# The last attention stage in pairs of heads, on halves of the TensorE array

## The chip, the cores and the metric

The kernel runs on one core of one Trainium2 chip. The metric is the device time of one launch in microseconds; a lower time is better. Everything is held in float32, and weights go to the array as a rounded part and a remainder (fp32r).

## The reference, cut to what matters

Two transformer layers follow one another on 512 tokens of width 1024. The first has a sparse and a windowed attention, the second a latent and a stick-breaking attention, and the third stage of attention, the one that is changed, is a causal softmax attention with forget gates: 16 heads of 64, for which

```python
q, k, v, gate logits = split(x @ w_in)          # 3 x 1024 + 16 columns
q, k   = rms_norm per head, times a gain of 64
decay  = cumsum(log_sigmoid(logits + f_bias))   # per head, over the tokens
s      = q @ k.T / 8 + decay[query] - decay[key]
p      = softmax(where(key <= query, s, -1e30))
out    = (p @ v) @ w_o
```

A feed-forward part closes each layer. The decay of the query is the same for all keys of a row, so a softmax does not see it.

## The kernel before, in words

The kernel is one program per engine, written in the order in which each engine runs it, with semaphores between them. TensorE (PE) does the products and transposes, ScalarE (ACT) copies and exponentials, VectorE (DVE) reductions and copies, GpSimd (POOL) splits each weight slab into high and low part (`split_slab`, two operations of 128x1024), SyncE issues the weight loads. Each phase (`in1`, `cmp`, ..., `in3`, `out3`, `up3`, `down3`) walks over slabs of weights; four slots hold split slabs.

`in3` projects to the queries, gate logits, keys and values of the last attention. Each chunk of 512 columns lands in `tok3` by tokens, is normed per head on DVE (`head_norms`), gets two more columns for the decays (`decays_beside`, so a head has 66), and is turned head by head by `pe_turn` (L603) into `qf` and `kf`, 66 rows by 512 tokens; ACT (L1189) and DVE (L1618) empty the banks in turn, with the gain.

The attention itself (`pe_attend`, `act_attend`, `dve_attend` with `att["fox"]`) goes over 16 heads, and in each over four blocks of 128 queries, the longest first: 512, 384, 256 and 128 keys. For each step PE forms the scores (L875; a float32 product is two loads of weights and two passes), adds the causal mask with a bf16 product (L880), three steps later turns the probabilities in blocks of 128x128 (L887), and then multiplies them with the values (L896, 64 columns out). DVE takes the negated row maximum (L1709), ACT the exponential with its sum (L1285) and the copy of the turned probabilities (L1298), DVE the inverse of the sum and the scaled result (L1730, L1923). POOL copies the queries of the next head into `q_st` (L456).

The result stands in `v3` by tokens. `pe_out` then turns it (L721, 32 transposes, name `x3`), ACT and DVE make the high and low part in `xt_hi` and `xt_lo` (L1122, L1550), and `out3` multiplies with the weights (L588 to L590).

At the very start `small_loads` has ACT issue 18 small loads; DVE waits for all of them (L1776), forms the rotation angles, ACT takes their sines, and only then ACT copies the first projected tiles (L1374).

Of the kernel before, what the change touches and what calls it, by code (L numbers as in the profile page):

```python
# [14 lines left out]
P = 128  # L15
SEQ = 512
D = 1024
NT = SEQ // P
# [8 lines left out]
TOKW = 528  # L27
# [3 lines left out]
SMALLS = 18  # L31
# [49 lines left out]
def build(nc, A, out):  # L81
# [17 lines left out]
    NORMS = ["n0", "n1", "n3", "n5", "x2", "n6", "n7", "x3", "n8"]  # L99
# [46 lines left out]
    band = sb("band", [P, P], BF16)  # L146
    one = sb("one", [P, 1])
# [13 lines left out]
    m_cos = sb("m_cos", [P, NT, ROPE])  # L161
    m_sin = sb("m_sin", [P, NT, ROPE])
# [68 lines left out]
    qf = sb("qf", [HD + 2, 16, SEQ], F32, u)  # L231
    kf = sb("kf", [HD + 2, 16, SEQ], F32, u)
# [5 lines left out]
    decay = sb("decay", [P, NT, 16], F32, u)  # L238
    u.close()
# [9 lines left out]
    red = sb("red", [P, NT, ROPE // 2], F32, u)  # L249
    u.close()  # L250
# [196 lines left out]

    def stage_queries(e, ph, q_src, rows, iters, ready, before=None):
# [25 lines left out]
    def _(e):  # L474
# [47 lines left out]
        e.wait_ge(consts, 19)  # L522
# [27 lines left out]
    def mla_heads(dst, h0, which):  # L550
# [14 lines left out]
    T_IN3 = [alternate([(66 * i, 66, (qf, kf)[c // 2][:, 8 * (c % 2) + i, :]) for i in range(8)],  # L565
                       g_col[0:66, 2 + c // 2:3 + c // 2]) for c in range(4)] + [[], []]
# [146 lines left out]
    def pe_to_xt(e, name, src, ready, t):  # L713

        e.wait_ge(*ready(t))
        for q in range(2):
            i = 2 * t + q
            if i >= 4 and name in ("n1", "x2", "x3"):
                e.wait_ge(*at(f"{name}_lo", i - 3))
# [49 lines left out]
    def pe_pairs(e, name, c, s0, kts, x_of, last, turn, when):  # L769
# [4 lines left out]
        for pair in ((0, 1), (2, 3)):  # L774
            for s, kt in enumerate(kts, s0):
# [4 lines left out]
                if pair[0] == 2:  # L780
                    m.then_inc(slab_used, 1)
                    for t in when.get(s - s0, ()) if turn else ():
                        turn(t)

# [78 lines left out]

    def pe_attend(e, cfg):
# [57 lines left out]
        with e.Fori(0, iters - 1) as j:  # L922
# [16 lines left out]
        "fox": dict(name="fox", iters=8, look=3, dh=HD + 2, band=False, mask=causal,  # L939
                    k=lambda hd: heads(kf, hd), v=lambda hd: columns(v3, hd),  # L940
                    start=[at("in3_tpa", 16), at("in3_tpd", 16), at("in3_copy", 23)], banks=[at("in3_copy", 24)]),
# [3 lines left out]
    def _(e):  # L945
# [108 lines left out]
        def decays():  # L1054

            e.wait_ge(*at("consts", 20))
# [6 lines left out]

        def turn_first():
            e.wait_ge(*at("fox_dec_out", 1))
# [5 lines left out]
                   "n7", turn("n7"), {(2, 0): turn_logits, (2, 1): decays, (2, 3): turn_first})  # L1071
        pe_attend(e, att["fox"])
# [967 lines left out]
```

## Time and profile before

| what | value |
|---|---|
| median of 3 runs | 2260.43 us (2259.78 to 2261.72) |
| span of the profiled execution | 2259.5 us |
| that execution's own time | within the runs' 2259.78 to 2261.72 us; the page gives its span alone |
| PE busy | 2103.5 us, 93% of the span |
| POOL, DVE, ACT busy | 1071.8, 894.1, 582.4 us |
| chain that ended last | PE 87%, DVE 7%, ACT 2% |
| last attention stage | 1745.5 to 1840.1 us |

A time is read from the start of the span. The length of an instruction includes its way through the engine; what one costs in a row of its kind is the distance from start to start. PE is the matmul itself, PEld the load of its weights, which can lie beside the matmul before.

### The profile page before, as it was taken

How to read it: one execution, taken by the hardware profiler on the slowest of the kernel's cores; microseconds unless marked ns; L12 is line 12 of the kernel's file. 1: busy time of each engine (PE TensorE's matmuls, PEld its weight loads, DVE VectorE, ACT ScalarE, POOL GpSimd, SP SyncE). 2: the span in 40 equal slices, each digit the busy share in tenths (PEclk: the TensorE clock that was granted, in tenths of full speed). 3: DMA queues.
4: the chain of work that ended last, by engine and by line, in shares of the span. 5: the costliest groups of instructions: out<-in, count | busy, mean ns of one | idle time of the engine just before them, and what ended most of it. 6: DMA issues, size and time to landing. Idle time of an engine off the chain costs nothing.

```text
span 2259.5 us, 30914 instructions
## 1 busy us (share of the span) xinstructions
PE 2103.5 (93%) x10410; PEld 1715.7 (76%) x10420; DVE 894.1 (40%) x1703; ACT 582.4 (26%) x1432; POOL 1071.8 (47%) x688
## 2 busy tenths in 40 slices
PE   5776999789999989879999999999999999999999
PEld 4665676678888878766678888887787888888887
DVE  4663567264434015546654221201362644221200
ACT  2111556232222003336532011100132642011100
POOL 4443003257666655400135666665553036666664
PEclk9887998889999999988579999999999999999999
DMA  4222001113333322110012333332221013333322
GB/s 132 66 61 66 0 0 38 47 57 111 93 95 119 93 77 82 54 38 1 0 47 84 103 98 97 93 94 84 79 85 62 1 38 94 103 101 94 94 94 91
DMA packets 125209, 161.90 MB, mean 72 GB/s; under 512 B 11511, under 2 KB 87239, under 8 KB 125127
## 3 DMA queue, kind: packets, MB, share of 16 engines
q1 hardware_dynamic: 121440, 159.97, 23.0%
q10 hardware_dynamic: 3686, 0.82, 0.2%
q8 instruction: 53, 0.87, 0.2%
q14 instruction: 30, 0.24, 0.0%
HBM read 158.66 MB, written 2.10 MB: 71 GB/s over the span
## 4 chain that ended last, share of the span: by engine, by line
PE 87%; DVE 7%; ACT 2%; issue 2%; DMA 1%; POOL 1%; ACTq 0%; SPq 0%; DVEq 0%; POOLq 0%
PE ps L588 22%; PE ps L589 22%; PE ps L590 22%; PE ps L875 7%; PE ps L896 5%; PE ps L887 3%; PE ps L603 2%; PE ps L721 2%; PE ps L880 1%; DVE tok L1540 1%; PE ps L903 1%; DVE xt_lo L1550 1%; PE ps L1003 1%; DVE rstd L1516 1%; ACT dump L1114 1%
## 5 line engine op out<-in xcount | busy, mean ns | idle before, releaser
L420 POOL TENSOR_TENSOR w_lo<-raw,w_hi 128x1024 fp32r<-128x1024 f32 (+1 forms) x256 | 616.6, 2409 | 21.3
L418 POOL TENSOR_SCALAR w_hi<-raw 128x1024 fp32r<-128x1024 f32 (+1 forms) x256 | 275.0, 1074 | 557.6 <-PE ps L590 536.7
L588 PE MATMUL ps<-xt_hi,w_hi 128*128 128x512 f32 (+1 forms) x1160 | 433.6, 374 | 7.2 <-DVE xt_lo L1550 6.5
L589 PE MATMUL ps<-xt_lo,w_hi 128*128 128x512 f32 (+1 forms) x1160 | 432.7, 373 | 0.0
L590 PE MATMUL ps<-xt_hi,w_lo 128*128 128x512 f32 (+1 forms) x1160 | 432.6, 373 | 0.0
L588 PE MATMUL ps<-w_hi,xt_hi 128*128 128x512 f32 (+3 forms) x672 | 264.6, 394 | 28.3 <-ACT tok L1374 18.3
L589 PE MATMUL ps<-w_lo,xt_hi 128*128 128x512 f32 (+3 forms) x672 | 260.4, 387 | 0.0
L590 PE MATMUL ps<-w_hi,xt_lo 128*128 128x512 f32 (+3 forms) x672 | 260.1, 387 | 0.0
L588 PEld LDWEIGHTS ps<-xt_hi,w_hi 128*128 128x128 f32 x1160 | 219.8, 189 | 47.4 <-DVE xt_lo L1550 7.6
L590 PEld LDWEIGHTS ps<-xt_hi,w_lo 128*128 128x128 f32 x1160 | 219.6, 189 | 38.5
L589 PEld LDWEIGHTS ps<-xt_lo,w_hi 128*128 128x128 f32 x1160 | 219.7, 189 | 38.2
L588 PE MATMUL ps<-w_hi,hid_hi 128*128 128x512 f32 x528 | 205.6, 389 | 0.0
L590 PE MATMUL ps<-w_hi,hid_lo 128*128 128x512 f32 x528 | 205.4, 389 | 0.0
L589 PE MATMUL ps<-w_lo,hid_hi 128*128 128x512 f32 x528 | 205.4, 389 | 0.0
L588 PEld LDWEIGHTS ps<-w_hi,xt_hi 128*128 128x128 f32 x672 | 131.4, 196 | 55.0 <-issue 24.1
L1684 DVE TENSOR_TENSOR tok<-ps,tok 128x512 f32<-128x512 f32 x44 | 30.4, 692 | 353.1 <-PE ps L590 353.1
L896 PE MATMUL ps<-v,prob_t 128*128 (+1 forms) x1072 | 162.2, 286 | 5.1 <-ACT prob_t L1298 3.6
L896 PEld LDWEIGHTS ps<-v,prob_t 128*128 128x128 f32 x1072 | 156.2, 214 | 7.5 <-ACT prob_t L1298 4.1
L590 PEld LDWEIGHTS ps<-w_hi,xt_lo 128*128 128x128 f32 x672 | 130.7, 195 | 24.2
L589 PEld LDWEIGHTS ps<-w_lo,xt_hi 128*128 128x128 f32 x672 | 131.2, 195 | 22.6
L432 POOL TENSOR_SCALAR w_hi<-raw 128x1024 fp32r<-128x1024 f32 (+5 forms) x48 | 45.8, 955 | 173.1 <-PE ps L590 162.7
L1235 ACT ACTIVATE tok<-ps 128x512 f32<-128x512 f32 x44 | 26.3, 598 | 356.3 <-PE ps L590 356.1
(268 smaller groups left out, 2799.1 us busy)
## 6 DMA issues: line engine op xcount, KB each, us to landing
raw<-in_w_up SPq DMA_DIRECT2D x88, 256.0 KB
raw<-in_l_w_gate SPq DMA_DIRECT2D x88, 256.0 KB
raw<-in_l_w_up SPq DMA_DIRECT2D x88, 256.0 KB
raw<-in_l_w_down SPq DMA_DIRECT2D x40, 512.0 KB
raw<-in_l_w_in SPq DMA_DIRECT2D x36, 512.0 KB
raw<-in_w_down SPq DMA_DIRECT2D x20, 512.0 KB
raw<-in_l_w_o SPq DMA_DIRECT2D x16, 512.0 KB
raw<-in_w_in SPq DMA_DIRECT2D x12, 512.0 KB
```

The source lines that it names most:

```text
L418: e.tensor_scalar(w_hi[:, s, 0:width], r, 1.0, 0.0, ALU.mult, ALU.add).then_inc(split, 1)
L420: e.tensor_tensor(w_lo[:, s, 0:width], r, w_hi[:, s, 0:width].bitcast(F32), ALU.subtract).then_inc(split, 1)
L432: e.tensor_scalar(view(w_hi[:, s, :]), view(raw[:, s % 2, :]), 1.0, 0.0, ALU.mult, ALU.add).then_inc(split, 1)
L588: e.matmul(o, s_hi, m_hi, start=start, stop=False)
L589: e.matmul(o, s_hi, m_lo, start=False, stop=False)
L590: return e.matmul(o, s_lo, m_hi, start=False, stop=stop)
L603: m = e.transpose(bank(ODD[i % 4], P, t * P, w), staged(name, c)[:, t, off:off + w], ident[:, :])
L721: m = e.transpose(bank(turn_bank(name, i), P, k * P), src(t)[:, (4 * q + k) * P:(4 * q + k + 1) * P], ident[:, :])
L875: e.matmul(o, q_st[0:cfg["dh"], hh, i * P:(i + 1) * P], cfg["k"](2 * j + hh)[:, k0 * P:k1 * P], start=True, stop=False)
L887: m = e.transpose(bank(4 + k % 2, P, x * P), prob[:, k % 4, x * P:(x + 1) * P], ident[:, :])
L896: m = e.matmul(bank(6 + k % 2, HD), prob_t[:, k % 2, x * P:(x + 1) * P], v(k0 + x), start=x == 0, stop=x == k1 - k0 - 1)
L1684: e.tensor_tensor(half_u[:, 2 * k + 1, :], bank((ODD, EVEN)[even][2 + k]), half_u[:, 2 * k, :], ALU.mult).then_inc(*od.done(*at(f"{name}_h ...
```

## The change

The last attention works on pairs of heads. `qf` and `kf` hold two heads in 128 rows, so `in3` turns 128 columns at once, and the two decay columns are gone. In their place the negated decays of the keys are split into three bf16 parts (`dk`, on DVE), turned once (`turn_decays`) into `ck_t`, and added to the scores by a bf16 product with a selecting matrix (`pick`). In `fox_scores` head 0 of a pair uses rows 0 to 63 of the array and head 1 rows 64 to 127, each into its own bank; the masks are done likewise on 64 rows, twice, the second time with the halves exchanged (`ident_x`, `causal_x`).

The probabilities are now divided by their sum before they are turned, by POOL (`pool_pairs`), in `tok` and `scratch`; four of `out3`'s slab splits stand between these. The transposes (L947 of the new kernel) take 64 queries at a time, from rows 0 to 63 into bank 4 and from rows 64 to 127 into bank 5. ACT and DVE copy them into `p_turn`, and the value product (L958) has the values as weights, 64 columns for each head, and streams 512, 384, 256 and 128 query columns, so its result is already turned. ACT and DVE take the high and low part of it (`high`, `low`); `x3` is gone and `out3` goes slab by slab (`pe_out_direct`).

```diff
@@ constants
-SMALLS = 18
+SMALLS = 20
+    ident_x = sb("ident_x", [P, P], BF16)
+    causal_x = sb("causal_x", [P, P], BF16)
-    qf = sb("qf", [HD + 2, 16, SEQ], F32, u)
-    kf = sb("kf", [HD + 2, 16, SEQ], F32, u)
+    qf = sb("qf", [P, 8, SEQ], F32, u)
+    kf = sb("kf", [P, 8, SEQ], F32, u)
+    p_turn = sb("p_turn", [P, 2, 2, 13, P], F32, u)
@@ POOL
+    def pool_pairs(e, name, pairs, slabs):
+        for g in range(4 * pairs):
+            if g in slabs:
+                split_slab(e, *slabs[g], SLAB)
+            e.wait_ge(*at(f"{name}_r", g + 1))
+            for x in range(2):
+                c = 2 * (g % 4) + x
+                e.tensor_scalar(prob_at(g, x), prob_at(g, x), den[:, c:c + 1], None, ALU.mult).then_inc(
+                    sem(f"{name}_w"), 1)
-        stage_queries(e, "fox", lambda hd: heads(qf, hd), HD + 2, 8,
-                      [at("in3_tpa", 16), at("in3_tpd", 16), (slab_used, 4 * (ph["in3"].g0 + 7))])
-        split_all(e, ph["out3"])
+        pool_pairs(e, "fox", 8, {2 + 5 * s: (ph["out3"].g0, s) for s in range(4)})
+        split_all(e, ph["out3"], 1)
@@ in3
-    T_IN3 = [alternate([(66 * i, 66, (qf, kf)[c // 2][:, 8 * (c % 2) + i, :]) for i in range(8)],
-                       g_col[0:66, 2 + c // 2:3 + c // 2]) for c in range(4)] + [[], []]
+    T_IN3 = [alternate([(P * i, P, (qf, kf)[c // 2][:, 4 * (c % 2) + i, :]) for i in range(4)],
+                       g_col[:, 2 + c // 2:3 + c // 2]) for c in range(4)] + [[], []]
@@ PE
+    def pe_pair_attend(e, cfg):
+        def scores(g):
+            if g >= 2:
+                e.wait_ge(*at(f"{name}_p", 2 * g - 2))
+            cfg["scores"](e, g // 4, 3 - g % 4, 2 * (g % 2)).then_inc(sem(f"{name}_s"), 1)
+        def turn_probs(g):
+            e.wait_ge(*at(f"{name}_w", 2 * g + 2))
+            if g:
+                for y in range(2):
+                    e.wait_ge(*is_turned(name, g - 1, y))
+            for kb in range(4 - g % 4):
+                for x in range(2):
+                    for y in range(2):
+                        r = slice(y * HD, (y + 1) * HD)
+                        m = e.transpose(bank(4 + y, HD, (2 * kb + x) * HD), prob_at(g, x)[r, kb * P:(kb + 1) * P],
+                                        ident[r, r])
+            m.then_inc(sem(f"{name}_t"), 1)
+        def values(p):
+            for kb in range(4):
+                for x in range(2):
+                    m = e.matmul(ps[x * HD:(x + 1) * HD, (6 + p % 2) * W + kb * P:(7 + p % 2) * W],
+                                 cfg["v"](p, x, kb),
+                                 cfg["p_turn"][:, p % 2, x, 4 * kb:3 * kb + 4, :].rearrange("p b n -> p (b n)"),
+                                 start=kb == 0, stop=kb == 3)
+        for g in range(steps_all + 4):
+            if g < steps_all:
+                scores(g)
+            if 3 <= g < steps_all + 3:
+                turn_probs(g - 3)
+            if g >= 7 and g % 4 == 3:
+                values((g - 7) // 4)
+    def fox_scores(e, p, i, b):
+        for x, r in enumerate(halves):
+            e.matmul(bank(b + x, n), qf[r, p, i * P:(i + 1) * P], kf[r, p, 0:n], start=True, stop=False)
+        for x, r in enumerate(halves):
+            e.matmul(bank(b + x, n), pick[r, p, :], ck_t[r, 0:n], start=False, stop=False)
+        for x, r in enumerate(halves):
+            e.matmul(bank(b + x, P, last), ident_b[r, :], causal[r, :], start=False, stop=False)
+        for x, r in enumerate(halves):
+            m = e.matmul(bank(b + x, P, last), ident_x[r, :], causal_x[r, :], start=False, stop=True)
-        pe_attend(e, att["fox"])
-        pe_out(e, "out3", "x3_lo", lambda t: pe_to_xt(e, "x3", lambda t: v3[:, t, :], lambda t: at("fox_ofree", 66), t),
-               turn("n8"), {1: (0,), 2: (1,)})
+        pe_pair_attend(e, att["fox"])
+        pe_out_direct(e, "out3", "fox_lo", turn("n8"), {1: (0,), 2: (1,)})
@@ DVE, the order in a step
+        for g in range(steps_all + 6):
+            if 4 <= g < steps_all + 4:
+                turned(g - 4)
+            if g < steps_all:
+                maxima(g)
+            if 1 <= g < steps_all + 1:
+                inverses(g - 1)
+            if g >= 9 and g % 4 == 1:
+                low((g - 9) // 4)
@@ small loads and start
+                if i >= 2:
+                    ld(g_col[HD:P, i:i + 1], src[0:HD].rearrange("(p o) -> p o", o=1))
+        for dst, src in ((ident_x, ident_b), (causal_x, causal)):
+            e.tensor_copy(dst[0:HD, :], src[HD:P, :]).then_inc(*od.own())
+            e.tensor_copy(dst[HD:P, :], src[0:HD, :]).then_inc(*od.own())
```

ACT copies bank 5 of the steps with 4 and 2 key blocks, DVE the other six half banks of a pair; ACT's order in a step is its copy, two exponentials, and once a pair `high`.

On PE, in the middle of the stage, one head of before reads as follows (`q_st` are the queries, `prob` and `prob_t` the probabilities before and after turning):

```order
L875 MATMUL ps<-kf,q_st 128x384
L880 MATMUL ps<-causal,ident_b 128x128
L885 REGISTER_ALU
L887 MATMUL ps<-ident,prob 128x128 x2
L896 MATMUL ps<-v,prob_t 128x64 x3
L875 MATMUL ps<-kf,q_st 128x256
L880 MATMUL ps<-causal,ident_b 128x128
```

And a part of a pair after the change, with the probabilities in `tok` and `scratch`:

```order
L984 MATMUL ps<-kf,qf 128x128 x2
L986 MATMUL ps<-ck_t,pick 128x128 x2
L988 MATMUL ps<-causal,ident_b 128x128 x2
L990 MATMUL ps<-causal_x,ident_x 128x128 x2
L947 MATMUL ps<-ident,tok 128x64 x16
L958 MATMUL ps<-p_turn,v 64x512 x2
L958 MATMUL ps<-p_turn,v 64x384 x2
L958 MATMUL ps<-p_turn,v 64x256 x2
L958 MATMUL ps<-p_turn,v 64x128 x2
L984 MATMUL ps<-kf,qf 128x512 x2
```

The value products have moved from every step to one block of eight after a pair's last step, each streaming up to 512 columns, and the transposes are four for each key block of a pair where they were two.

On PE, where the stage ends and `out3` begins, before:

```order
L887 MATMUL ps<-ident,prob 128x128
L896 MATMUL ps<-v,prob_t 128x64 x3
L721 MATMUL ps<-ident,v 128x128 x16
L588 MATMUL ps<-w_hi,xt_hi 128x512
L589 MATMUL ps<-w_lo,xt_hi 128x512
```

And after:

```order
L958 MATMUL ps<-p_turn,v 64x256 x2
L958 MATMUL ps<-p_turn,v 64x128 x2
L624 MATMUL ps<-w_hi,xt_hi 128x512
L625 MATMUL ps<-w_lo,xt_hi 128x512
```

The transposes of `x3` (L721) no longer stand between the last value product and the first product of `out3`.

On POOL, the first steps of the stage after the change, with a slab split among the multiplications:

```order
L476 TENSOR_SCALAR tok<-tok,den 128x512 x2
L476 TENSOR_SCALAR tok<-tok,den 128x384
L476 TENSOR_SCALAR scratch<-scratch,den 128x384
L426 TENSOR_SCALAR w_hi<-raw 128x1024
L428 TENSOR_TENSOR w_lo<-raw,w_hi 128x1024
L476 TENSOR_SCALAR tok<-tok,den 128x256 x2
```

Before, POOL had only the copies of the queries (L456) there, and the splits behind them.

## Rows read from the trace of the kernel before

**Rows 1.** The page: the span, and the granted clock in 40 slices of 56.5 us.

```profile
span 2259.5 us, 30914 instructions
...
PEclk9887998889999999988579999999999999999999
```

**Rows 2.** Busy time by stretch: start:end, length, PE, PEld, DVE, ACT, POOL, clock, DMA.

```profile
1745.47:1840.10 94.63, 94.24 (x679) 75.70 (x680) 57.32 (x190) 63.79 (x192) 22.61 (x23) 1.00 0.06 17
```

**Rows 3.** Groups by line and shape in the stage: busy us, mean ns of one.

```profile
L1709 DVE TENSOR_REDUCE nmax<-ps 128x1 f32<-128x512 f32 x16 | 11.1, 692 | 36.7 <-PE ps L880 36.7
L1285 ACT ACTIVATE prob<-ps,nmax 128x512 f32<-128x512 f32 x16 | 11.0, 687 | 2.2 <-DVE nmax L1709 2.2
...
L1709 DVE TENSOR_REDUCE nmax<-ps 128x1 f32<-128x384 f32 x16 | 8.9, 558 | 2.3 <-PE ps L880 0.3
```

**Rows 4.** Timeline of PE in one head: start us, length us, instructions.

```profile
1755.98 1.08 PE L875 MATMUL ps<-kf,q_st 66*128 x2
...
1756.90 0.22 PE L880 MATMUL ps<-causal,ident_b 128*128 128x128 bf16 x1
...
1756.96 0.49 PE L887 MATMUL ps<-ident,prob 128*128 128x128 f32 x3
...
1757.29 1.00 PE L896 MATMUL ps<-v,prob_t 128*128 x8
...
1758.13 0.86 PE L875 MATMUL ps<-kf,q_st 66*128 x2
```

**Rows 5.** Timeline, POOL's copy for the next head: first attention stage, last attention stage.

```profile
264.62 0.61 POOL L456 COPY q_st<-qt 64x512 f32 x1 [6.11 <-PE ps L880]
...
1824.75 0.61 POOL L456 COPY q_st<-qf 66x512 f32 x1 [5.14 <-PE ps L880]
```

**Rows 6.** Timeline, weight loads of four small transposes each, in `in1`.

```profile
73.90 0.33 PEld L950 LDWEIGHTS ps<-ident,c_raw 44*128 44x128 f32 x4 [0.35 <-issue]
74.28 0.20 PEld L953 LDWEIGHTS ps<-ident,pe_raw 16*64 16x64 f32 x4
```

**Rows 7.** Timeline, the 32 transposes of one chunk in `in3`.

```profile
1642.18 3.66 PE L603 MATMUL ps<-ident,tok 128*66 128x128 f32 x32
```

**Rows 8.** Timeline, PE from `in3` into the stage.

```profile
1744.02 0.39 PE L589 MATMUL ps<-w_lo,xt_hi 128*128 128x512 f32 x1
...
1744.24 0.39 PE L590 MATMUL ps<-w_hi,xt_lo 128*128 128x512 f32 x1
...
1745.47 1.12 PE L875 MATMUL ps<-kf,q_st 66*128 66x512 f32 x2 [0.84 <-POOL q_st L456]
```

**Rows 9.** Timeline, PE from the stage into `out3`, and its second block of transposes.

```profile
1839.83 0.41 PE L896 MATMUL ps<-v,prob_t 128*128 128x64 f32 x2 [0.15 <-DVE v L1923]
...
1843.57 0.47 PE L588 MATMUL ps<-w_hi,xt_hi 128*128 128x512 f32 x1 [0.79 <-DVE xt_lo L1550]
...
1848.86 0.39 PE L590 MATMUL ps<-w_hi,xt_lo 128*128 128x512 f32 x1
...
1849.10 1.91 PE L721 MATMUL ps<-ident,v 128*128 128x128 f32 x16
...
1850.76 0.48 PE L588 MATMUL ps<-w_hi,xt_hi 128*128 128x512 f32 x1
```

**Rows 10.** Timeline, the start: a small load's issue, DVE's first step, POOL's last split.

```profile
46.19 0.62 ACTq L1082 DMA_DIRECT2D g_col<-in_l_fox_k_norm  x1
...
49.34 1.06 DVE L1776 TENSOR_SCALAR neg_sink<-sink 128x8 f32<-128x8 f32 x1 [11.03 <-DMA w_sb<-in_cmp_w]
...
58.74 2.42 POOL L434 TENSOR_TENSOR w_lo<-raw,w_hi 128x1024 fp32r<-128x1024 f32 x1
```

**Rows 11.** Waits of PE from 30 to 90 us: total, times, longest.

```profile
PE ps L588 <- ACT tok L1374: 11.2, 1, 11.2
```

**Rows 12.** Busy time by stretch, as in rows 2, in the stick-breaking attention.

```profile
1054.00:1057.00 3.00, 1.42 (x7) 0.71 (x6) 2.90 (x5) 1.32 (x3) 0.00 (x0) 1.00 0.00 0
1057.00:1060.00 3.00, 2.24 (x9) 1.23 (x8) 2.86 (x8) 2.61 (x7) 0.00 (x0) 0.54 0.00 0
```

More of the change, by code:

```diff
@@ L717, in pe_to_xt @@
             i = 2 * t + q
-            if i >= 4 and name in ("n1", "x2", "x3"):
+            if i >= 4 and name in ("n1", "x2"):
                 e.wait_ge(*at(f"{name}_lo", i - 3))
@@ L783, in pe_pairs, with pe_out_direct @@
                         turn(t)
+    def pe_out_direct(e, name, lo, turn_next, when):
+        for s in range(4):
+            e.wait_ge(split, 2 * (4 * phases[name].g0 + s) + 2)
+            e.wait_ge(*at(lo, 2 * s + 2))
+            for t in range(NT):
+                m = slab_tile(e, name, 0, s, OUT_KTS[s], x_model, KD - 1, t)
+            m.then_inc(slab_used, 1)
+        pe_pairs(e, name, 1, 0, OUT_KTS, x_model, KD - 1, turn_next, when)
     def pe_out(e, name, xt, turn_in, turn_next, when):
@@ L862, in ahead, with turner, is_turned, turned_probs @@
             stage(j + 1, k - 8)
+    def turner(g, y):
+        return "a" if y == 1 and g % 2 == 0 else "d"
+    def is_turned(name, g, y):
+        k = turner(g, y)
+        n = sum(turner(gg, yy) == k for gg in range(g + 1) for yy in range(2) if (gg, yy) <= (g, y))
+        return at(f"{name}_pt{k}", n)
+    def turned_probs(cfg, g, y):
+        i = 3 - g % 4
+        return cfg["p_turn"][:, g // 4 % 2, :, i:4 * i + 1:3, y * HD:(y + 1) * HD].rearrange("p x b n -> p b x n")
+    def turned_bank(g, y):
+        return bank(4 + y, (4 - g % 4) * P).rearrange("p (b x n) -> p b x n", x=2, n=HD)
@@ new lines, in fox_scores @@
+    def fox_scores(e, p, i, b):
+        n, last = (i + 1) * P, i * P
+        halves = (slice(0, HD), slice(HD, P))
+        for x, r in enumerate(halves):
[6 more added lines that the diff above has]
+            m = e.matmul(bank(b + x, P, last), ident_x[r, :], causal_x[r, :], start=False, stop=True)
+        return m
@@ L938, in build @@
                     banks=[at("att2_ofree", 34)]),
-        "fox": dict(name="fox", iters=8, look=3, dh=HD + 2, band=False, mask=causal,
-                    k=lambda hd: heads(kf, hd), v=lambda hd: columns(v3, hd),
-                    start=[at("in3_tpa", 16), at("in3_tpd", 16), at("in3_copy", 23)], banks=[at("in3_copy", 24)]),
+        "fox": dict(name="fox", pairs=8, scores=fox_scores, p_turn=p_turn,
+                    v=lambda p, x, kb: v3[:, kb, (2 * p + x) * HD:(2 * p + x + 1) * HD],
+                    start=[at("in3_tpa", 8), at("in3_tpd", 8), at("in3_copy", 23), at("picks", 6), at("fox_ck", 1)],
+                    banks=[at("in3_copy", 24)]),
     }
@@ L1500, in _ @@
             act_turned(e, od, "in3", plan, c)
-        act_attend(e, od, att["fox"])
-        for t in range(NT):
-            act_high(e, od, "x3", t)
+        act_pair_attend(e, od, att["fox"])
         act_out(e, od, "out3", "n8")
```

144 lines of the change are left out of this document (120 added, 24 removed).

## The prediction

> **What bounds the kernel now.** I read the page first: one core, a span of 2259.5 us, and a granted TensorE clock of 9 or 10 tenths in nearly every slice [rows 1]. The runs' median, 2260.43 us, lies 0.9 us above that span. The sum below is made on the span, and I carry the same 0.9 us to the forecast. The reader should see that PE is what ends last almost everywhere, so the next question is what fills PE in the stage that is rewritten. By stretches, the last attention stage runs from 1745.47 to 1840.10 us: 94.63 us, of which PE is busy 94.24, DVE 57.32, ACT 63.79, POOL 22.61, at a clock of 1.00 [rows 2]. That is PE-bound, with no engine near it. Inside it, POOL's copy for the next head returns after 5.14 us of waiting and 0.61 of work, so one head takes 5.75 us and a pair 11.5 [rows 5]; 16 heads are 92, and 2.6 are ends.
>
> What PE does in one head is seen in [rows 4]. The product for 512 keys starts at 1755.98 and the mask at 1756.90: 0.92 us, two passes of 0.43 each (0.107 per 128 columns) and some 0.06. The bf16 mask over 128 columns takes 0.06. Three transposes run from 1756.96 to 1757.29, 0.11 each. Four value products, eight passes, run from 1757.29 to 1758.13, 0.105 a pass: each streams only 64 columns, so loading 128 columns of weights is what costs there.
>
> **The change, part by part.** Most is in the stage itself, the rest lies around it.
>
> *Turning Q and K in in3.* A chunk now turns 32 blocks of 66 columns in (3.66 - 0.27) / 31 = 0.109 us each [rows 7]; four chunks are 128. They become 64 blocks of 128 columns, each again streaming 128 columns of identity: 64 x 0.109 = 7.0 us less on PE. ACT and DVE empty half as many banks, so they cannot hold it up more. The new turn of the decays is 4 transposes, +0.5. Its DVE steps stand behind the forget gates, while PE has a slab of 24 x 0.225 = 5.4 us [rows 8]; bounds 0 and +2 for a wait there, taken 0.
>
> *Start of the stage.* PE's last in3 products start at 1744.02 and 1744.24, so one streams for some 0.225 and the last ends at 1744.47; and the scores start at 1745.47 because POOL copies queries until then [rows 8]. Those copies go: -1.0.
>
> *Between the stage and out3.* The last value product starts at 1839.83 and is streamed by 1840.05; out3 starts at 1843.57. Later 16 more transposes hold PE from 1849.10 (the product before it starts at 1848.86 and streams 0.225) to 1850.76 [rows 9]. All 32 are gone, since the value product now leaves its result transposed: -3.5 - 1.7 = -5.2. The split of the last pair is needed only by out3's fourth slab, 16 us in, which hides it.
>
> *The start of the kernel.* This one costs. Two more small loads are issued by ACT at 0.62 us each, ahead of the load for which DVE waits until 49.34; four more copies stand on DVE [rows 10]. DVE's chain from there to the sines is held up by POOL's splits, the last of which ends at 58.74 + 2.42 = 61.16, and PE then waits 11.2 us for ACT's first copy behind the sines [rows 11]. So the delay arrives on PE whole. The shift is 1.24 + some 0.8; part of it vanishes in the gaps between POOL's splits. I take +1.2; bounds +0.5 and +2.5.
>
> Around the stage: -7.0 + 0.5 - 1.0 - 5.2 + 1.2 = -11.5.
>
> *The stage.* No row of before shows two half arrays at work at once, so it is bounded from both sides. For a pair of heads the four steps hold 4, 3, 2 and 1 key blocks, 10 in all.
>
> If halves overlap: PE takes products in order, so head 0's second pass runs beside head 1's first, and scores cost three passes for four: 3 x 10 x 0.107 = 3.2; one bf16 run of the decays, 10 x 0.053 = 0.5; four masks a step at 0.05 to 0.06, 0.8; sum 4.5. There are 40 half transposes of 128 weight columns. Four such loads in a row (44 rows high) take 0.33 with 0.14 of the last, 0.063 apart, and half as wide ones 0.031 [rows 6]; with halves beside each other I take 0.031: 1.3. Values: two heads, two passes over 1280 columns, 4 x 1.07 = 4.3 in a line, 2.6 overlapped with the unpaired end. Sum 8.4.
>
> If they do not: scores 4.3 + 1.1 + 1.0 = 6.4, transposes 40 x 0.063 = 2.5, values 4.3: 13.2.
>
> Both get the change of shape between half and whole rows. The first attention stage works on 64 rows for its scores, this one on 66; a head returns every 6.11 + 0.61 = 6.72 us against 5.75 [rows 5]. That is 0.97 over four visits to the 64-row shape, 0.24 a visit. The new stage keeps scores, masks and transposes on half rows and leaves them once a pair: +0.24. The Trainium skill (TensorEngine Tiling, Key Properties) says that changing the tiling mode, not just the tile, drains TensorE; by that rule the difference between the two stages has a cause, and the trace agrees with 0.24 us.
>
> So PE has 8.6 us of work a pair, overlapped, where it had 11.5. The gain of 23 us does not arrive, since **waits take PE's place**. The banks of the transposes (4 and 5) are single, and a step must wait for both copies of the step before. DVE's order is copies, then the reduction of the new scores. A reduction over 512 columns is 0.692 and over 384 0.558 [rows 3], so over 2 x 512 it is 1.23. After the four-block scores, DVE needs 0.2 + 1.23 + 0.1 for the inverse + two copies of 384 (0.47 and 0.55) = 2.55 before the two-block transposes may start. PE has 0.38 of transposes and 1.32 of scores in that time: it waits 0.85. Then the three-block reduction (0.96) starts late by as much, ACT's two exponentials (0.55 each; 0.69 is the length at 512) follow, and only behind them ACT's own copy: PE waits about 0.95 again before the one-block transposes, and some 0.3 at smaller places. That is 2.1 a pair. ACT's and DVE's own sums, 5 and 6 to 7 us a pair, are under it, and POOL's multiplications (0.61 for 512, from its copy [rows 5]) make 3.6. The four slab splits of 3.5 us in POOL's queue lie one in five steps, with two to three steps of slack before PE asks; taken 0, bound +4.
>
> Stage: 8 x (8.6 + 2.1) = 86, and 5 for filling and emptying the pipeline (2.6 before; at the end no scores lie between the steps, so each chain of exponential, inverse, multiplication, transpose and copy is waited for in full): 91, against 94.6, so **-4**. Total 2260.4 - 11.5 - 4 = 2245.
>
> At this place the Trainium skill speaks against the change: TensorEngine Tiling, PSUM Bottleneck, says that tiling speeds up TensorE but not the emptying of PSUM, which may become the bound. By that rule nothing is left of PE's gain in the stage. The sum above gives it a sixth, since here the copies bind only at two steps in four; by the rule alone the time would be 2249.
>
> **Rivals.**
> 1. *Halves do not overlap.* For: nothing in the profile shows that they do. Against: a 64-row product behaves as a shape of its own in [rows 5], so the array does tell its halves apart; that is why I give this the smaller chance. PE then has 13.4 and waits under 1 a pair: 8 x 14 + 5 = 117, +22 in the stage, total 2271. If the row halves overlap and only the column halves of the value product do not, it is some +10 on my forecast: 2255. The forecast turns slower where a pair costs over 12.7 us. The Trainium skill (TensorE: Matmul & The Clock Gate, The mechanism) has products on different row groups start 4 ns apart, and 3.07 times the speed for four of them; no row here shows it.
> 2. *The clock falls.* In the stick-breaking stage PE was busy 1.42 of 3 us between 1054 and 1057, the granted clock fell to 0.54 [rows 12], and the page's slice from 1073 to 1130 stands at 5 tenths although PE looks fully busy [rows 1]. That is 1.2 for 2.4 GHz, and passes take twice as long. For: the new stage has two waits of near 1 us a pair, between steps that use half the rows. Against: that gap was 1.6 us and the new ones are shorter, and the value products are long dense streams. If it falls at each pair and returns with the values, 4 us a pair come on top: 2245 + 32 = 2277; if once or twice, 2250 to 2255.
> 3. *The queues beside PE are longer than summed*, by 0.5 to 1 us a pair (a late inverse, a POOL split in the way, strided writes of the copies): 4 to 8 us, 2249 to 2253. The skill's PSUM rule above ends in this rival.
> 4. *It does nothing around the stage*: not likely, since each of those terms is a stretch on PE that is read off directly; in the other direction, waits half as long as I add give 2237.
>
> **How the numbers follow.** Overlap with a clock that stays, 0.58, gives 2239 to 2250, most likely 2245. Rival 3 has 0.10, the column half of rival 1 has 0.06 (2255), no overlap has 0.11 (2266 to 2280), the clock 0.15 (half under 2256, half above). The range 2238 to 2268 leaves out 0.02 below and the larger part of "no overlap" and of the worst clock case above, some 0.17. A difference within 0.2% (4.5 us) is about what a measurement of this kernel cannot tell from no change. Faster by over that, under 2255.9: 0.58 + 0.10, half of 0.06 and a little of the clock case, less 0.03 for a startup that costs more, 0.70. Within it, up to 2264.9: 0.08. Slower: 0.22.
>
> **What would show it.** In the profile after, head 1's first pass should start within about 0.05 us of head 0's second, and 16 half transposes take 0.5 us; if the first takes the end of the second instead, rival 1 holds. The stage should last about 91 us with DVE's and ACT's copies as the ones PE waits for before two transposes in four. in3's transposes should number 64, out3 should begin with no gap, and PE's wait for ACT near 54 to 65 us should be about 12.4 instead of 11.2. The clock in the stage's stretches should be 1.00. I am wrong if a pair takes over 12.7 us, or if the clock shows 0.5 there.

## The result: no gain, and what the profile after shows

The changed kernel takes 2263.14 us (median of 12 runs, 2260.14 to 2270.29); the kernel before, run beside it on the same chip, 2259.84 (12 runs, 2255.51 to 2262.08). The ratio is 1.0017, 95% interval 1.0009 to 1.0025. The forecast was 2245. The time lies in the forecast's range of 2238 to 2268, but in the case "within 0.2%", which had a chance of 0.08.

The profiled run is the slowest of the twelve (2270.29, span 2268.6). Its page first; the clock row answers to [rows 1].

```profile
span 2268.6 us, 30201 instructions
...
PEclk9887998889999999998589999999999889999999
```

The stage now starts at 1739.00 and `out3` at 1850.31: 111.3 us, where the kernel before had 94.6 [rows 2] and the forecast 91. Busy time by stretch, columns as in [rows 2]:

```profile
1739.00:1850.31 111.31, 82.18 (x777) 46.79 (x777) 51.93 (x119) 46.69 (x152) 81.50 (x72) 0.80 0.07 20
```

The reader sees three things. PE's work really fell, although its passes run at a mean clock of 0.80. POOL, which had 22.61 us here, has 81.50. And the clock, 1.00 before, is 0.80. The groups of POOL in the stage say where its time goes:

```profile
L476 POOL TENSOR_SCALAR tok<-tok,den 128x512 f32<-128x512 f32 x16 | 24.8, 1563 | 22.1 <-DVE den L1926 22.1
L476 POOL TENSOR_SCALAR tok<-tok,den 128x256 f32<-128x256 f32 x16 | 14.6, 923 | 0.0
L476 POOL TENSOR_SCALAR tok<-tok,den 128x384 f32<-128x384 f32 x8 | 9.9, 1242 | 0.0
...
L428 POOL TENSOR_TENSOR w_lo<-raw,w_hi 128x1024 fp32r<-128x1024 f32 x4 | 9.4, 2349 | 0.3
...
L476 POOL TENSOR_SCALAR tok<-tok,den 128x128 f32<-128x128 f32 x8 | 4.8, 602 | 15.1 <-DVE den L1926 15.1
L426 POOL TENSOR_SCALAR w_hi<-raw 128x1024 fp32r<-128x1024 f32 x4 | 4.2, 1047 | 0.0
```

A multiplication of 512 columns takes 1.56 us, not the 0.61 that I took from the copy in [rows 5]. A pair has 2 x (1.563 + 1.242 + 0.923 + 0.602) = 8.66 us of them, eight pairs 69, and the four slab splits 13.6 more.

The timeline of PE in a stretch of the stage (start, length) shows the halves and both kinds of wait:

```profile
1761.59 1.13 PE L984 MATMUL ps<-kf,qf 64*128 64x512 f32 x4
1762.55 0.38 PE L986 MATMUL ps<-ck_t,pick 64*128 64x512 bf16 x2
...
1762.88 0.23 PE L947 MATMUL ps<-ident,tok 64*128 64x64 f32 x2
...
1763.26 0.87 PE L984 MATMUL ps<-kf,qf 64*128 64x384 f32 x4
...
1765.45 0.46 PE L947 MATMUL ps<-ident,tok 64*128 64x64 f32 x8 [1.04 <-DVE p_turn L1932]
...
1767.86 0.37 PE L947 MATMUL ps<-ident,tok 64*128 64x64 f32 x2 [1.08 <-ACT p_turn L1458]
...
1768.10 0.77 PE L984 MATMUL ps<-kf,qf 64*128 64x128 f32 x4
1768.63 0.34 PE L986 MATMUL ps<-ck_t,pick 64*128 64x128 bf16 x2
...
1770.58 1.12 PE L947 MATMUL ps<-ident,tok 64*128 64x64 f32 x16 [1.39 <-POOL tok L476]
1771.62 3.77 PE L958 MATMUL ps<-p_turn,v 128*64 128x512 f32 x16
```

The float32 scores of both heads over 512 keys take 0.96 us (1761.59 to 1762.55), where one head took 0.92 with its rows alone [rows 4]: the halves overlap. Twelve half transposes take 0.38 (1762.88 to 1763.26). The waits of 1.04 and 1.08 us for DVE's and ACT's copies are those of the forecast. The wait of 1.39 us for POOL is not. Behind it the 16 value passes take 3.71 us (1771.62 to 1775.33) at a mean granted clock of 0.61; they take 2.31 where the clock is 1.00 (below). In this pair the clock had fallen already ahead of that wait: four score passes over 128 keys take 0.53 us (1768.10 to 1768.63), against 0.28 at a clock of 1.00 (run 9). The pairs before had waited up to 2.76 us for POOL.

### The profile page after: what moved, and what is told of

It reads as the page before. It is cut to its first block, busy times and chain, and to the rows that moved or that the text cites. A ratio compares the mean times of both kernels' runs of the same rounds, so it can differ in the third digit from the quotient of the medians.

```text
span 2268.6 us, 30201 instructions
## 1 busy us (share of the span) xinstructions
PE 2078.8 (92%) x10414; PEld 1675.3 (74%) x10424; DVE 880.5 (39%) x1592; ACT 555.8 (25%) x1376; POOL 1128.7 (50%) x743
## 4 chain that ended last, share of the span: by engine, by line
PE 83%; DVE 8%; POOL 4%; ACT 2%; issue 2%; DMA 1%; ACTq 0%; SPq 0%; DVEq 0%; POOLq 0%
PE ps L624 22%; PE ps L626 21%; PE ps L625 21%; PE ps L1004 5%; PE ps L1025 4%; PE ps L1016 2%; POOL tok L476 2%; PE ps L639 2%; PE ps L757 1%; DVE tok L1708 1%; PE ps L958 1%; PE ps L1009 1%; POOL w_lo L428 1%; PE ps L1032 1%; DVE xt_lo L1718 1%
## 5 line engine op out<-in xcount | busy, mean ns | idle before, releaser
L1025 PE MATMUL ps<-v,prob_t 128*128 (+1 forms) x752 | 119.9, 296 | 4.5 <-ACT prob_t L1436 3.4
L1025 PEld LDWEIGHTS ps<-v,prob_t 128*128 128x128 f32 x752 | 115.9, 225 | 6.5 <-ACT prob_t L1436 3.1
L625 PEld LDWEIGHTS ps<-w_lo,hid_hi 128*128 128x128 f32 x528 | 99.1, 188 | 20.7
```

The source lines that it names most:

```text
L625: e.matmul(o, s_hi, m_lo, start=False, stop=False)
L1025: m = e.matmul(bank(6 + k % 2, HD), prob_t[:, k % 2, x * P:(x + 1) * P], v(k0 + x), start=x == 0, stop=x == k1 - k0 - 1)
```

## The experiments

Theory A: POOL's multiplications, 2.5 times as long as priced, are what the stage waits for. Theory B: the halves or the copies cost more than summed, and POOL only lies beside them. Theory C: the clock falls by itself in work on half rows. The ratios are to the kernel before on the same chip. "Stage" is from the first score to `out3`'s first product; "clock" is the mean granted clock over it, from the profile of each run.

| kernel | median us | ratio, 95% | stage us | clock |
|---|---|---|---|---|
| changed | 2263.14 | 1.0017 (1.0009-1.0025) | 111.3 | 0.80 |
| 1 no division | 2238.98 | 0.9909 (0.9891-0.9928) | 84.7 | 1.00 |
| 2 constant factor | 2257.35 | 0.9984 (0.9965-1.0003) | 105.0 | 0.82 |
| 3 all on ACT | 2263.11 | 1.0020 (1.0010-1.0030) | 111.2 | 0.79 |
| 4 all on DVE | 2266.72 | 1.0031 (1.0020-1.0043) | 114.7 | 0.76 |
| 5 two operations | 2241.86 | 0.9938 (0.9924-0.9951) | 91.0 | 0.92 |
| 6 filler products | 2256.50 | 0.9987 (0.9977-0.9996) | 103.5 | 0.92 |
| 7 diagonal | 2269.60 | 1.0057 (1.0043-1.0071) | 114.5 | 0.90 |
| 8 slabs after the stage | 2257.55 | 0.9994 (0.9984-1.0003) | 104.9 | 0.80 |
| 9 slabs moved | 2238.39 | 0.9904 (0.9888-0.9921) | 84.7 | 1.00 |
| 10 other copies | 2240.47 | 0.9915 (0.9900-0.9930) | 84.6 | 1.00 |
| 11 full-row transposes | 2246.94 | 0.9941 (0.9927-0.9954) | 90.8 | 0.98 |
| 12 slabs moved, filler | 2237.08 | 0.9896 (0.9881-0.9912) | 85.1 | 1.00 |

**1. No division.**

```diff
-                e.tensor_scalar(prob_at(g, x), prob_at(g, x), den[:, c:c + 1], None, ALU.mult)...
-            e.wait_ge(*at(f"{name}_w", 2 * g + 2))
+            e.wait_ge(*at(f"{name}_r", g + 1))
```

> The changed kernel with POOL's 64 multiplications of the last attention stage left out, so the probabilities are not divided by their row sums; PE's transposes wait for DVE's inverses instead. Everything else stands. Theory A (POOL's multiplications, 8.66 us a pair where PE has about 8.6 of work, are what PE waits for, and with POOL's four slab splits of 3.4 us they fill the stage): the stage falls from 111 us to 86 to 92, the granted clock in it rises to above 0.95, and the time is 2238 to 2246 us. Theory B (the halves cost PE more than summed, or the copies of the banks 4 and 5 bind, and POOL only lies beside it): the stage stays over 105 and the time over 2256. Theory C (the granted clock falls by itself in work on half rows): the clock stays at 0.8 although the waits are gone, and the time is 2250 to 2256.

Theory A holds, B and C fall; the stage, 84.7 us, is even shorter than A's 86 to 92. (This kernel and the next leave the division out and serve only to time the rest.) The clock is 1.00 in the whole stage, and from one pair's value passes to the next it is 10.2 us six times, and 6.1 for the last. Busy time, columns as before:

```profile
1735.50:1820.20 84.70, 65.13 (x778) 39.57 (x777) 51.73 (x119) 45.62 (x152) 13.59 (x8) 1.00 0.09 26
```

**2. A constant factor**, to see what makes a multiplication dear.

```diff
-                e.tensor_scalar(prob_at(g, x), prob_at(g, x), den[:, c:c + 1], None, ALU.mult)...
+                e.tensor_scalar(prob_at(g, x), prob_at(g, x), 1.0, None, ALU.mult)...
```

> The changed kernel, but POOL multiplies by the constant 1.0 where it had the column of inverses, so the division by the row sums is left out in value; number, sizes and order of all instructions are the same. If the per-row operand is what makes a multiplication cost 1.56 us for 512 (POOL's copy of the same size took 0.61), it falls to 0.55 to 0.65, the stage to 86 to 93 us and the time to 2240 to 2247. If any multiplication with float32 on POOL costs 1.56, this kernel is as the changed one: 2260 to 2266.

Neither forecast came out whole. The column of inverses costs little: 512 columns still take at most 1.49 us (the view of that line: shortest, median, longest).

```profile
L476 POOL TENSOR_SCALAR tok<-tok x48: 526/1008/1492, 1737.3 to 1831.6; 128x512 f32<-128x512 f32 x16, 128x256 f32<-128x256 f32 x16, 128x384 f32<-128x384 f32 x8, 128x128 f32<-128x128 f32 x8
```

POOL's busy time in the stage falls from 81.5 to 76.2 us and the stage by 6.3, which speaks for POOL deciding there. One of the ten executions stands apart: nine took 2253.3 to 2260.2 us at a mean granted clock over the whole program of 0.934 to 0.937, and one took 2238.09 at 0.947, the time of run 1. No trace of it was kept, but it hints that with a clock that stays up this POOL work costs little (see run 6). Run 2 also showed where to look: a slab split's `w_hi` takes 1.05 us for 1024 columns, and it is the same instruction with two operations.

**3 and 4. The multiplications on ACT, on DVE.**

```diff
+                e.activation(prob_at(g, x), prob_at(g, x), ACT.Copy, scale=den[:, c:c + 1])...   # 3
+                e.tensor_scalar(prob_at(g, x), prob_at(g, x), den[:, c + x:c + x + 1], None, ALU.mult)...   # 4
```

> The changed kernel with all 64 multiplications on ACT, after its exponentials and copies of the step before; POOL has the slab splits alone. ACT then has 8 us a pair (exponentials and sums 4.4, copies 1, the splitting copy 0.6, multiplications some 3), close to PE's 8.6. Theory A: the stage is 90 to 98 us and the time 2243 to 2251. Theory B: over 2256, since ACT's copies of bank 5 come later than before.

> The changed kernel with all 64 multiplications on DVE, right behind its inverses; POOL has the slab splits alone. DVE then has 5 us a pair and some 2.5 to 4 for the multiplications, 8 to 9 us, in the order reduction, inverse, multiplications, copies. Theory A: stage 90 to 100 us, time 2244 to 2254. Theory B: over 2258, since the copies for which PE waits stand behind more work.

Both miss: I expected 90 to 100 us and got 111.2 and 114.7, with POOL nearly idle. So theory A in its narrow form (POOL alone) does not tell all. Waits of PE on the matmul side, from 1735 to 1845, multiplications on ACT:

```profile
PE ps L943 <- ACT p_turn L1454: 21.2, 8, 2.9
PE ps L943 <- DVE p_turn L1937: 8.1, 8, 1.2
```

ACT has 73.3 us of work in 111.2 and is not full; but its copy stands behind exponentials and multiplications, and PE waits up to 2.9 us for it once a pair, as long as it waited for POOL. The clock falls again (0.79 and 0.76). So an engine's sum does not tell whether it holds the others up: what stands behind the multiplication in its queue counts too. A multiplication in the chain (scores, reduction, exponentials, inverse, multiplication, transposes, copy) is not what costs by itself, since run 5 has one of 1.4 us for both heads at 512 columns there, as ACT has, and loses nothing in an undisturbed pair. How much of 111.2 and 114.7 is the queue and how much the fallen clock was not tried.

**5. Two operations.** The result is the same number, the form is that of the slab splits.

```diff
-                e.tensor_scalar(prob_at(g, x), prob_at(g, x), den[:, c:c + 1], None, ALU.mult)...
+                e.tensor_scalar(prob_at(g, x), prob_at(g, x), den[:, c:c + 1], 0.0, ALU.mult, ALU.add)...
```

> The changed kernel, with POOL's multiplication written with two operations (times the inverse, plus 0.0) instead of one, the form that the slab splits have: those take 1.05 us for 1024 columns, where the multiplication with one operation takes 1.56 for 512 (and 1.49 with a constant in place of the column). Theory A1 (the form of the instruction sets POOL's price): the multiplication falls to 0.55 to 0.65 us for 512, POOL's work in a pair from 8.66 to about 3.5, the stage from 111 us to 84 to 92, and the time to 2240 to 2250. Theory A2 (POOL needs 1.5 us for any product with one source read and written in place): it stays at 1.5, the stage over 105, the time 2258 to 2266.

A1 holds. Groups of POOL in this kernel's stage (busy us, mean ns):

```profile
L476 POOL TENSOR_SCALAR tok<-tok,den 128x512 f32<-128x512 f32 x16 | 10.9, 691 | 25.8 <-DVE den L1926 25.8
...
L476 POOL TENSOR_SCALAR tok<-tok,den 128x256 f32<-128x256 f32 x16 | 7.5, 477 | 0.2
L476 POOL TENSOR_SCALAR tok<-tok,den 128x384 f32<-128x384 f32 x8 | 4.7, 585 | 2.7 <-DVE den L1926 2.7
...
L476 POOL TENSOR_SCALAR tok<-tok,den 128x128 f32<-128x128 f32 x8 | 3.0, 372 | 22.8 <-DVE den L1926 22.8
```

0.69 instead of 1.56, 4.25 us a pair instead of 8.66. The stage takes 91.0 us, the length forecast. The kernel is 16.9 us faster than the one before between the medians (2258.77 beside it), 14.0 us by the ratio; the forecast was 15.4. So one changed operation takes away the whole miss of 20.3 us in the stage. The two profiled spans differ by more, 30.2 us: in this run 6.1 fewer lie ahead of the stage and 3.8 behind it, which has other causes (below). That the stage is 91 to the tenth is partly luck: an undisturbed pair takes 10.2 instead of 10.7, the ends 3 instead of 5, and the slab splits 6 instead of nothing (run 9).

**6. Filler products** of two times 512 bf16 columns ahead of each step's transposes in the changed kernel.

```diff
+                for _ in range(2):
+                    e.matmul(bank(6 + v % 2), ident_b[:, :], dump[:, 0:W], start=True, stop=True)
```

> The changed kernel with two bf16 products of 512 columns (0.43 us at the full clock), whose result nobody reads, ahead of the wait of each step's transposes from the third pair on. Theory A (POOL's queue of 83 us in the stage and the latency of its 3.1 us at the four-block step bind; the lower clock follows from the waits and adds some 5 to 8 us): the clock rises to above 0.9 and the time falls to 2254 to 2260, not further. Theory C (the clock is what makes the stage long, and POOL is hidden): the clock rises and the time falls to 2245 or less. If the waits are long enough for the clock to fall anyway, the clock stays near 0.8 and the time is 2263 or more.

The time is the one that theory A gave, and the ratio falls by 0.0030, about 7 us. But this is only the least that the fallen clock costs, since the products did not hold it up throughout: its mean is 0.88 over the first 73 us of the stage, with 0.67 from 1780 to 1790, and it is 1.00 from 1790 on. There two pairs without a slab split can be compared with two such pairs of the changed kernel (busy time from value pass to value pass, columns as before; changed kernel first, filler second):

```profile
1811.97:1838.22 26.25, 21.09 (x197) 12.04 (x193) 13.04 (x30) 11.58 (x38) 17.47 (x17) 0.76 0.00 1
1806.92:1828.62 21.70, 19.50 (x210) 10.43 (x209) 12.97 (x30) 11.57 (x38) 17.06 (x17) 1.00 0.01 2
```

POOL's multiplications are the same, 1.56 us for 512 columns. A pair takes 13.1 us at the low clock and 10.85 at the full one, filler included, where it takes 10.2 without any division (run 1). So of the 2.9 us that such a pair loses, at most 0.6 is POOL's time itself and 2.3 come with the fallen clock. The whole stage says the same: against run 1, PE is busy 82.2 us instead of 65.1 with the same products, 17 of the 26.6 us by which the stage is longer. Only in the first five pairs, with their four slab splits, would POOL bind at any clock: 5 x 8.66 + 4 x 3.4 = 56.9 us where the pairs need 51. That is some 6 us, an estimate. So theory A has the cause, since run 5 shows that without POOL's long multiplications the excess goes; but most of what they cost arrives by way of the clock that falls behind the waits. No run held the clock up through the whole stage, so the exact shares stay open.

**7. Diagonal.** The division inside the transposes, as a float32 product with a diagonal of inverses.

```diff
-                        m = e.transpose(bank(4 + y, HD, (2 * kb + x) * HD), prob_at(g, x)[...], ident[r, r])
+                        m = e.matmul(bank(4 + y, HD, (2 * kb + x) * HD), prob_at(g, x)[...], inv_d[r, g % 4, x, :],
+                                     start=True, stop=True)
```

> The changed kernel without any multiplication of the probabilities: each transpose becomes a float32 product with a diagonal matrix of the inverses, which DVE builds for both heads in one instruction of 128 columns behind its inverse. PE then turns in two passes instead of one: the 40 half transposes of a pair (1.3 us) become about 2.6, so PE's work is 9.5 to 10 a pair, and the wait between exponentials and transposes is some 0.4 us instead of POOL's 1.2 to 3.1. Theory A: the stage is 86 to 94 us at a clock of 1.00 and the time 2243 to 2252. Theory B (the copies of banks 4 and 5, or the rest of the chain, are what binds): over 2256.

Missed, because of my price for PE. Its timeline at a clock of 1.00:

```profile
1813.14 0.39 PE L946 MATMUL ps<-inv_d,tok 64*128 64x64 f32 x4
...
1814.48 0.87 PE L983 MATMUL ps<-kf,qf 64*128 64x384 f32 x4
...
1819.79 2.00 PE L946 MATMUL ps<-inv_d,tok 64*128 64x64 f32 x32 [0.23 <-DVE p_turn L1937]
1821.72 2.37 PE L957 MATMUL ps<-p_turn,v 128*64 128x512 f32 x16
```

The turning of a three-block step takes 1.34 us (1813.14 to 1814.48) against 0.38 as transposes (above), the four-block one 1.93 (1819.79 to 1821.72) against 0.64 in run 1. Two passes cost three times a transpose, not twice. An undisturbed pair takes 12.2 us, and the clock fell in the stretches with slab splits. Whether the rest of 114.5 comes from the splits alone was not tried.

**8 and 9. The slab splits.** First behind the stage in the changed kernel; then, with the multiplication of two operations, at other steps:

```diff
-        pool_pairs(e, "fox", 8, {2 + 5 * s: (ph["out3"].g0, s) for s in range(4)})
+        pool_pairs(e, "fox", 8, {})                                                   # 8, and all four splits behind it
+        pool_pairs(e, "fox", 8, {7 + 4 * s: (ph["out3"].g0, s) for s in range(4)})    # 9
```

> The changed kernel with POOL's four slab splits (3.4 us each) moved from the stage to behind it. Theory A: POOL's queue in the stage falls from 83 to 69 us, which takes 4 to 10 us out of the stage; but out3 then waits for its first slab, 3.4 us, and for each of the next, since PE takes 5.4 us a slab and POOL 3.5, only the first counts: net 2256 to 2262. If the splits lay in POOL's slack, the stage stays at 111 and the time is 2266 or more.

> The kernel with the two-operation multiplication, and POOL's four slab splits put ahead of the one-block step of the pairs 1 to 4 (before steps 7, 11, 15, 19 instead of 2, 7, 12, 17), where POOL stands idle for 4.5 us in an undisturbed pair. In the kernel with the splits at the old places the pairs took 10.2, 11.8, 12.6, 10.2, 10.2, 10.2 us, so the splits cost about 4 us in the stage with the clock that falls behind them (0.72 between 1770 and 1780). If the collision is the cause, all pairs take 10.2 and the time falls by 3 to 5 us to 2237 to 2239; if the splits were not what those pairs waited for, it stays at 2242.

Both hit. I had priced the splits' place at nothing. They cost 6.4 us in the changed kernel's stage and 6.3 in the one with two operations: its pairs took 10.2, 11.8, 12.6, 10.2, 10.2 and 10.2 us, and now all take 10.2. The median falls by less, 3.5 us, since in the profile of run 5 the stretch behind the stage happened to be 3.5 us shorter than in that of run 9 ("From the stage to `out3`", below). POOL's timeline in an undisturbed pair of run 5 shows a slot that fits:

```profile
1793.23 0.93 POOL L476 TENSOR_SCALAR tok<-tok,den 128x256 f32<-128x256 f32 x2
1798.65 0.37 POOL L476 TENSOR_SCALAR tok<-tok,den 128x128 f32<-128x128 f32 x1 [4.49 <-DVE den L1926]
```

4.49 us idle before each pair's last step, room for the 3.4 of a split. In run 9 the stage is 84.7 us, as without any division, with the clock at 1.00:

```profile
1734.19:1818.86 84.67, 65.05 (x777) 39.61 (x777) 51.67 (x119) 45.56 (x152) 46.70 (x72) 1.00 0.08 26
```

**10. Other copies.** ACT takes both halves of the three-block step's transposes and its half of the two-block ones ahead of its exponentials.

```diff
-        return "a" if y == 1 and g % 2 == 0 else "d"
+        return "a" if g % 4 == 1 or y == 1 and g % 2 == 0 else "d"
```

> As the kernel with the late slab splits, and the two copies that PE still waits for in each pair (1.04 us before the two-block and 1.08 us before the one-block transposes) are taken from behind DVE's reduction of the four-block scores: ACT copies both halves of the three-block transposes and its half of the two-block ones ahead of its next exponentials, and DVE's splitting copy stands one step later. My account of the waits (the banks 4 and 5 are single, and the copies stand in line behind a reduction) expects 0.8 to 1.6 us less a pair: 2225 to 2233. If instead PE waits for the multiplied probabilities by then, or ACT's queue becomes the bound, the pair stays at 10.2 and the time at 2237 to 2241.

Most of the waits for the copies went and others took their place (PE's waits from 1744 to 1814, seven pairs: total, times, longest):

```profile
PE ps L984 <- ACT tok L1451: 6.3, 7, 0.9
PE ps L984 <- ACT scratch L1451: 4.5, 7, 0.7
PE ps L947 <- DVE p_turn L1934: 3.9, 7, 0.6
```

PE now waits 1.5 us a pair for exponentials to free the score banks and 0.6 for copies: 2.1, nearly the 2.35 of before. The pair takes 10.4 instead of 10.2, and the time, 2240.47, is that of my alternative, ACT's queue. ACT is busy only 51.5 of 84.6 us, so it is the order in its queue and not its sum. That the chain through reduction and exponentials is the limit, whichever engine copies, fits this and was not shown by a run of its own.

**11. Full-row transposes**, with two operations and the slab splits at the old places.

```diff
-                    for y in range(2):
-                        ...
+                    m = e.transpose(bank(4 + x, P, kb * P), prob_at(g, x)[:, kb * P:(kb + 1) * P], ident[:, :])
```

> The kernel with the two-operation multiplication, but its transposes are done over all 128 rows (20 a pair of 128 columns, head 0 into bank 4 and head 1 into bank 5) instead of 40 on row halves. Scores and masks stay on halves, values on column halves. From the rows 20 full transposes cost 0.109 each, 2.2 us a pair, where 16 half ones take 0.64, so 40 take 1.6; and the array changes between halves and full rows four times a pair instead of once, 0.24 each. That is +0.6 and +0.7: 1.3 a pair at most, less what falls into waits: 2245 to 2253. If the halves of the transposes are worth nothing, 2240 to 2243.

An undisturbed pair takes 10.6 us against 10.2, so row halves are worth 0.4 us a pair in the transposes. The ratio, 0.9941, cannot be told from the 0.9938 of run 5. PE's own work grew by 1.4 us, as the sum of 1.3 had it (10.64 less waits of 0.47 and 0.92, against 7.85 below), but 1.0 of it fell into the waits for copies: the one before the two-block step is 0.47 us instead of 1.04. The stage is no longer than in run 5 because its clock is 0.98, not 0.92; why it fell less was not tried. The 1.4 us hold three more changes of shape and some 0.6 for the longer transposes, so they fit the 0.24 us a change of the prediction without measuring it.

**12. Slabs moved, one filler product a step.**

> As the kernel with the late slab splits, and one bf16 product of 512 columns (0.21 us) ahead of each step's transposes from the third pair on. If the granted clock is at 1.00 through the stage without it, the products cost what of them is not hidden in the two waits of a pair, 0.2 to 0.5 us a pair: 1 to 4 us more than without, 2239 to 2243. If the clock still falls somewhere in the stage without them, they give back 2 to 5 us.

0.9896 against 0.9904 without: no difference, where I expected 1 to 4 us more. With a clock of 1.00 in the stage there is nothing to give back. Runs 9 and 12 are the fastest versions found, 1.0% under the kernel before.

## Why the prediction was wrong

**The step that failed** is the term "POOL's multiplications (0.61 for 512, from its copy [rows 5]) make 3.6 a pair". They make 8.66. The copy is another instruction, without arithmetic. The trace of before had POOL's split to `w_hi`, a `tensor_scalar` too, 1024 columns in 1.05 us, but with two operations; no row of it has the form with one. So this price was unknown and should have had a bound from above; I gave it none. With two operations, 4.25 a pair, the stage is what was forecast (run 5). The Trainium skill (GPSIMD Engine Reference, Engine selection) calls elementwise work with one input on this engine roughly line-rate; the rows agree for the form with two operations and not for that with one, three times slower. I gave the case rival 3, "the queues beside PE are longer", and a price of 0.5 to 1 us a pair; it was 2.5. POOL's 8.66 us still fit into the 10.2 of an unhindered pair, and with the clock up they cost at most 0.6 (run 6); but the first five pairs, with the slab splits, give it more than they need themselves, and the clock fell behind the waits for POOL.

**"The four slab splits ... taken 0, bound +4"**: they cost 6 us in both forms of the kernel. They lay, as I had said, "in one in five steps", and that was the fault: only one step in four has the idle slot.

**"The clock falls"** (rival 2, 0.15) came true as a consequence, and carries the larger part of the loss: 2.3 of 2.9 us in the two pairs compared in run 6, and at least 7 us in all. The two waits of near 1 us a pair that I feared do not bring it down (1.00 throughout in runs 1, 9 and 12); with the waits for POOL beside them, 14.4 us in the stage and up to 3.05 at once, it falls. It does not take a long one: the fall that shows at 1822.23 follows waits of 1.28, 1.01, 1.04 and 1.08 us, of which only the second is for POOL.

**The halves overlap**, as forecast. Scores, pair by pair at 512 keys, 0.96 us; values 2.31 at the full clock where I summed 2.6; 16 half transposes 0.64 where I expected 0.5. PE's own work in an undisturbed pair is 10.2 - 1.04 - 1.08 - 0.23 = 7.85 us (forecast 8.6), and its waits for copies 2.35 (forecast 2.1, at the two steps named). The Trainium skill's rule in TensorEngine Tiling, PSUM Bottleneck, that emptying PSUM may become the bound, is borne out in part: these 2.35 us are such waits, but in runs 1 and 9 10 us of gain are left in the stage (84.7 against 94.6).

**Before the stage** the forecast was -6.3 and the profile shows 1745.47 to 1739.00, -6.5. The twelve experiments, whose code is the same up to there (run 7 has one more POOL step), start the stage at 1732.4 to 1736.5. So the start differs by up to 6.6 us between profiled runs, the match of -6.5 is in part luck, and the small terms cannot be told apart. Of those, the wait for POOL's queries is gone. The startup term (+1.2) is not shown: PE's wait near 60 us grew from 11.2 [rows 11] to 12.7, but DVE's step behind the sines starts at 63.44, where it started at 64.00, and PE goes on at 65.46, where it went on at 66.02.

**From the stage to `out3`** there is no gap, and all 32 transposes are gone: -5.2, as forecast. But from `out3`'s start to the end the profiled run takes 418.3 us, where 415.9 less 1.7 was due: 4.1 more. Timeline of DVE, POOL and PE in that stretch, first the kernel before, then the changed one:

```profile
1894.62 0.16 DVE L1516 SCALAR_TENSOR_TENSOR rstd<-sq_a,rstd 128x2 f32<-128x2 f32 x1
1894.82 3.26 DVE L1540 SCALAR_TENSOR_TENSOR tok<-h,rstd,gains 128x1024 f32<-128x1024 f32 x2
...
1895.00 2.01 POOL L418 TENSOR_SCALAR w_hi<-raw 128x1024 fp32r<-128x1024 f32 x1 [1.50 <-DMA raw<-in_l_w_up]
```

```profile
1899.65 0.99 DVE L1684 SCALAR_TENSOR_TENSOR rstd<-sq_a,rstd 128x2 f32<-128x2 f32 x1
1900.67 4.68 DVE L1708 SCALAR_TENSOR_TENSOR tok<-h,rstd,gains 128x1024 f32<-128x1024 f32 x2
...
1899.59 1.05 POOL L426 TENSOR_SCALAR w_hi<-raw 128x1024 fp32r<-128x1024 f32 x1 [1.05 <-DMA raw<-in_l_w_up]
1900.72 2.35 POOL L428 TENSOR_TENSOR w_lo<-raw,w_hi 128x1024 fp32r<-128x1024 f32 x1
...
1904.21 1.97 PE L757 MATMUL ps<-ident,tok 128*128 128x128 f32 x8 [2.54 <-DVE tok L1708]
```

PE did not wait there before. DVE's small step of 0.16 us now takes 0.99 and ends with POOL's `w_hi`, 1.05 from 1899.59, at 1900.64; before, POOL's split began only behind that step. The two steps of 128x1024 take 4.68 instead of 3.26. The Trainium skill (SBUF — State Buffer, Who interferes with whom) has an instruction of DVE with two inputs in SBUF contend with one of POOL that reads there, and the rows agree. Nine of the twelve experiments have PE's wait, 2.1 to 2.6 us; run 5 has 0.3, runs 3 and 10 none. In those three `out3`'s start to the end takes 414.2 to 414.5 us, the 414.2 that was due, and in the nine 416.4 to 418.2. So the 4.1 go with this wait, and it seems to hang on where POOL's splits, which follow the loads, happen to fall. That was read from the rows and not tried.

The sum of the misses on the span: 20.3 in the stage, 4.1 behind it, -0.2 ahead of it: 24.2 of the 24.5 between 2244.1 (2245 less the 0.9 beside the span) and 2268.6. Between the medians the miss is 18.

## What to carry to other kernels

Price an instruction by a row of the same form, not of the same engine and size: where there is none, the price is unknown (here it was 2.5 times too low), and the range should hold that, above all for an instruction that stands in the chain of every step. Add up each engine pair by pair beside the new length, not as an average beside the old one: a pair with a slab split gives POOL 8.66 + 3.4 = 12.1 us, over the 10.7 that the forecast has. Ask of each new wait whether the clock will follow it down, since that can cost more than the wait itself. And place work that only fills a queue into the slot where the trace shows that queue idle.

## What the runs showed of the hardware

- POOL's `tensor_scalar` with one operation takes 0.60, 0.92, 1.24 and 1.56 us for 128, 256, 384 and 512 float32 columns, 2.5 ns a column; with a second operation that does nothing (+ 0.0), 0.37, 0.48, 0.58 and 0.69, 0.83 ns a column. The column operand against a constant is worth 0.07 us.
- Two float32 products on the two row halves run together: 0.96 us for both heads, 0.92 for one.
- A float32 product of 64 columns on half rows takes three times a transpose of the same blocks (1.93 against 0.64 us for 16).
- Two waits of 1.04 and 1.08 us in a pair of 10.2 left the granted clock at 1.00 through the stage; with waits for POOL of up to 3.05 us beside them it fell to a mean of 0.80. The same pair of heads with the same work on POOL took 13.1 us at a mean clock of 0.76 and 10.85 at 1.00 with two filler products a step.
